# A two-block model in one program: no products of zeros ahead of the experts, and the six key and value units made among the experts all taken from the second layer

## The reference, cut to what matters

```
def hierarchical_moe(h, ...):                       # 256 tokens, D = 1024, 32 experts of 512
    y = jnp.zeros((B * S, D), jnp.float32)
    for e in range(N_EXPERTS):
        hid = jax.nn.silu(t @ w1[e]) * (t @ w3[e])
        y = y + comb[:, e:e + 1] * (hid @ w2[e]).astype(jnp.float32)

def memory_cross_attention(h, mem_n, w_q, w_kv, w_o):
    q = (h @ w_q).reshape(B, S, XATTN_HEADS, XATTN_HEAD_DIM)
    k, v = jnp.split(mem_n @ w_kv, 2, axis=-1)      # 256 x 1024 each, per layer
    ...

for l in range(DEPTH_2):                            # two layers
    x = x + FFN_RES_WEIGHT * swiglu_ffn(...)
    proj = rms_norm(x, mix_norm_g[l]) @ w_mix_in[l]
    y_rwkv = rwkv7_time_mix(...)                    # 8 heads
    y_moba = moba_attention(q_m, k_m, v_m, rel_bias)# 8 heads, one block of 256
    x = x + jnp.concatenate([y_rwkv, y_moba], axis=-1) @ w_mix_out[l]
    x = x + memory_cross_attention(rms_norm(x, xattn_norm_g[l]), rms_norm(mem, mem_norm_g[l]), ...)
    x = x + FFN_RES_WEIGHT * swiglu_ffn(...)
```

## Time and profile before

| | us |
|---|---|
| median of 3 runs (2256.39 to 2260.35) | 2259.84 |
| the profiled execution's own time | 2262.87 |
| its span, first to last instruction | 2261.1 |
| PE busy in the span | 2184.8 (97%) |
| DVE busy | 1240.1 (55%) |
| ACT busy | 426.6 (19%) |
| experts, pair 0's first product to the last scatter | 353.6 to 837.6 |
| head loop of layer 0, first transpose to last value product | 1172.1 to 1195.9 |
| head loop of layer 1 | 1874.9 to 1898.7 |

### The profile page before, as it was taken

One profiled execution on the slowest core, in us unless ns is written; L12 is line 12 of the kernel. 1 busy time (PEld: TensorE's weight loads), 2 busy tenths in 40 slices (PEclk: granted clock), 3 DMA queues, 4 the chain that ended last, 5 costly groups with the idle time before them and its releaser, 6 DMA issues.

```text
span 2261.1 us, 29957 instructions
## 1 busy us (share of the span) xinstructions
PE 2184.8 (97%) x12564; PEld 1481.3 (66%) x12564; DVE 1240.1 (55%) x2258; ACT 426.6 (19%) x858; POOL 50.5 (2%) x85
## 2 busy tenths in 40 slices
PE   7999999999999989999999999999999999999998
PEld 5778853433333337866968678856884976687873
DVE  2798422101110126676777766667666867767675
ACT  1123321101000012101142321101210132322110
POOL 1000100000000000000000000000000000000000
PEclk9999999999999999999999999999999999999999
DMA  9655587999999995444341435436453423245441
GB/s 406 266 223 232 223 277 303 421 421 421 422 421 421 421 390 161 163 168 167 113 163 45 149 122 174 162 130 214 159 181 135 168 83 125 78 151 182 159 181 42
DMA packets 174318, 499.98 MB, mean 221 GB/s; under 512 B 7128, under 2 KB 99560, under 8 KB 143984
## 3 DMA queue, kind: packets, MB, share of 16 engines
q1 hardware_dynamic: 169664, 481.23, 56.3%
q0 software_dynamic: 4384, 16.43, 2.2%
q10 hardware_dynamic: 144, 0.52, 0.1%
HBM read 491.34 MB, written 6.82 MB: 220 GB/s over the span
## 4 chain that ended last, share of the span: by engine, by line
PE 85%; DMA 9%; DVE 4%; ACT 1%; issue 1%; SPq 0%; POOL 0%; DVEq 0%; POOLq 0%
PE bank L2510 23%; PE bank L2558 11%; DMA ring<-in_w 8%; PE bank L1528 6%; PE bank L952 6%; PE bank L2623 6%; PE bank L1569 3%; PE bank L3053 2%; PE bank L2871 2%; PE bank L3126 2%; PE bank L1619 2%; PE bank L942 1%; PE bank L1056 1%; PE bank L1087 1%; PE bank L2602 1%; PE bank L1553 1%
## 5 line engine op out<-in xcount | busy, mean ns | idle before, releaser
L2510 PE MATMUL bank<-Tw,Sx 128*128 128x256 f32 x1032 | 229.9, 379 | 0.0
L2510 PEld LDWEIGHTS bank<-Tw,Sx 128*128 128x128 f32 x1032 | 193.0, 190 | 24.6
L1989 DVE TENSOR_TENSOR sg<-sg,bank 128x512 f32<-128x512 f32 x16 | 11.0, 688 | 283.4 <-PE bank L1528 283.4
L2510 PE MATMUL bank<-ring,xT 128*128 128x256 f32 x688 | 155.5, 379 | 0.0
L2510 PEld LDWEIGHTS bank<-ring,xT 128*128 128x128 f32 x688 | 130.5, 190 | 18.0 <-issue 0.5
L952 PE MATMUL bank<-xT,ring 128*128 128x256 f32 x640 | 141.8, 380 | 0.0
L952 PEld LDWEIGHTS bank<-xT,ring 128*128 128x128 f32 x640 | 120.7, 190 | 19.0 <-issue 3.3
L1528 PE MATMUL bank<-ring,xg 128*64 128x512 f32 x512 | 114.5, 594 | 18.5 <-DMA ring<-in_w 18.5
L1569 PE MATMUL bank<-ring,hTg 128*64 128x512 f32 x512 | 113.4, 595 | 0.0
L3550 DVE TENSOR_TENSOR whole<-bank,part 128x256 f32<-128x256 f32 (+1 forms) x133 | 57.5, 432 | 99.5 <-PE bank L2510 98.4
L2558 PE MATMUL bank<-Tw,Sx 128*128 128x512 f32 x240 | 108.9, 592 | 0.0
(11 more groups left out here) (643 smaller groups left out, 3761.6 us busy)
## 6 DMA issues: line engine op xcount, KB each, us to landing
ring<-in_w SPq DMA_DIRECT2D x128, 1024.0 KB, 23.9
ring<-in_ffn_w_in SPq DMA_DIRECT2D x88, 1024.0 KB, 7.7
ring<-in_first_pieces SPq DMA_DIRECT2D x33, 2048.0 KB, 11.9
more<-in_w SPq DMA_DIRECT2D x48, 1024.0 KB, 23.6
ring<-in_ffn_w_out SPq DMA_DIRECT2D x20, 2048.0 KB, 7.8
ring<-in_w_mix_in SPq DMA_DIRECT2D x12, 2048.0 KB, 7.9
ring<-in_xattn_w_kv SPq DMA_DIRECT2D x5, 2048.0 KB, 7.9
spare<-in_w SPq DMA_DIRECT2D x8, 1024.0 KB, 26.3
```

What stands on the lines that cost most here:

```text
L2510: last = nc.tensor.matmul(bank[BANK_OF[name]][:, 0:SEQ], lhs(k), rhs(k), start=(k == 0), stop=(k == 3))
```

## The change

`EARLY` now holds units 0 to 5 of layer 1, at steps 2 to 7. So `LEFT` becomes (0, 1, 2, 3, 6, 7) for layer 0 and (6, 7) for layer 1. `ALONE` is 4 in layer 0 and 2 in layer 1: layer 0 has one more whole unit ahead of the head loop and two units in it, where it had one; in layer 1 the second unit is the one in two halves, around `bonus` and the two `mats`, and the head loop has none. Layer 0 loads three pieces of `xattn_w_kv`, layer 1 one (before, two and two). Step 0 of the experts is written out apart on PE without anything to scatter in pair 0; the first scatter, in pair 1, opens the banks itself (`start=True`).

```diff
-EARLY = ((0, 0, 1), (0, 1, 2), (1, 0, 3), (1, 1, 4), (1, 2, 5), (1, 3, 6))
+EARLY = ((1, 0, 2), (1, 1, 3), (1, 2, 4), (1, 3, 5), (1, 4, 6), (1, 5, 7))
...
-            pe.wait_ge(kv_act, 2)
-            pe.wait_ge(ye_dve, 2)
-            for b in range(4, 8):
-                last = nc.tensor.matmul(bank[b][:, :], ye[:, 0, 0:P], ye[:, 1, :], start=True, stop=False)
-            last.then_inc(scattered, 1)
-            for lo, hi, first, l, keys in EARLY_SEGMENTS:
+            for q in range(2):
+                up(0, q)
+                if q == 1:
+                    pe.wait_ge(ye_dve, 2)
+                    gather(1, 0, (0, 1))
+                    scatter(0, 0, 0, start=True)
+                turn(0, q)
+                if q == 1:
+                    scatter(0, 1, 1)
+                    pe.wait_ge(hT_ready, 2)
+                    pe.wait_ge(whotT_ready, 2)
+                    gather(1, 1, (2, 3))
+                down(0, q)
+            for lo, hi, first, l, keys in EARLY_SEGMENTS[1:]:
...
-            for half in range(2):
-                nc.vector.memset(ye[:, half, :], 0.0).then_inc(ye_dve, 1)
-            nc.vector.memset(whotT[:, 1, :], 0.0).then_inc(whotT_ready, 1)
             weighted(0)
...
-        ALONE = [4 if len(t) > 4 else 3 for t in LEFT]
+        ALONE = [4 if len(t) > 4 else len(t) // 2 + 1 for t in LEFT]
...
                 scores(0)
-                cross_kv(l, LEFT[l][1])
+                cross_kv(l, LEFT[l][1], range(0, KD if ALONE[l] > 2 else 4))
                 bonus(l)
                 if ALONE[l] == 4:
                     cross_kv(l, LEFT[l][2])
                 pe.wait_ge(fac_ready, l + 1)
                 mats(l, 0)
-                cross_kv(l, LEFT[l][ALONE[l] - 1], range(0, 4))
+                if ALONE[l] > 2:
+                    cross_kv(l, LEFT[l][ALONE[l] - 1], range(0, 4))
                 mats(l, 2)
                 cross_kv(l, LEFT[l][ALONE[l] - 1], range(4, KD))
```

More of the change, by code:

```diff
@@ L150 @@
         EARLY_SEGMENTS.append((_i, _i + 1, _u, _l, _g < 4))
-_full, _at = [], 0
+_full, _at = [(0, 1, None, None, None)], 1
+assert EARLY[0][2] > 0
 for _s in EARLY_SEGMENTS + [(PAIRS // 2, PAIRS // 2, None, None, None)]:
@@ L1511, in up @@
                 for m in range(2):
-                    if m == 1:
-                        pe.wait_ge(whotT_ready, n + 1)
+                    if m == 1 and not (isinstance(n, int) and n == 0):
+                        pe.wait_ge(whotT_ready, n)
                         if taken is not None:
@@ L1545, in turn, with scatter @@
                 last.then_inc(whotT_psum, 1)
-            def scatter(par, turn_, done, stop=False):
-                pe.wait_ge(scattered, done)
+            def scatter(par, turn_, done, start=False, stop=False):
+                if start:
+                    pe.wait_ge(kv_act, 2)
+                else:
+                    pe.wait_ge(scattered, done)
                 for e in range(2):
@@ L1553, in scatter @@
                         last = nc.tensor.matmul(bank[4 + 2 * t + half][:, :], whotT[r, par, t * P:(t + 1) * P],
-                                                ye[r, half, :], start=False, stop=stop)
+                                                ye[r, half, :], start=start, stop=stop)
                 last.then_inc(scattered, 1)
@@ L1601, in tensor_gathered @@
                         if first is not None and q == 0:
-                            pe.wait_ge(whotT_ready, n + 2)
+                            pe.wait_ge(whotT_ready, n + 1)
                             early_products(pe, xT, i + (first - lo + 1), l, keys)
-            pe.wait_ge(whotT_ready, PAIRS + 1)
-            pe.wait_ge(ye_dve, 2 * PAIRS + 2)
+            pe.wait_ge(whotT_ready, PAIRS)
+            pe.wait_ge(ye_dve, 2 * PAIRS)
             for turn_ in range(2):
-                scatter((PAIRS + 1) % 2, turn_, 2 * PAIRS + turn_ + 1, stop=turn_ == 1)
+                scatter((PAIRS + 1) % 2, turn_, 2 * PAIRS + turn_ - 2, stop=turn_ == 1)
             for _ in range(6):
@@ L2002, in vector_gathered @@
                 if t == 0:
-                    dve.wait_ge(scattered, 2 * PAIRS + 3)
+                    dve.wait_ge(scattered, 2 * PAIRS)
                 for half in range(2):
@@ L2074, in build @@
         KEYS_LEFT = [sum(g < 4 for g in t) for t in LEFT]
-        KV_PLACES = [{4: (0, 1, 2, 3), 3: (0, 1, 3), 2: (0, 3)}[len(t) // 2] for t in LEFT]
+        KV_PLACES = [{4: (0, 1, 2, 3), 3: (0, 1, 3), 2: (0, 3), 1: (0,)}[len(t) // 2] for t in LEFT]
         assert all(t[0::2] == [g - 1 for g in t[1::2]] for t in LEFT)
@@ L3313, in take_kv @@
                     nc.scalar.activation(dst, bank[g % 2][:, :], ACT.Copy).then_inc(kv_act, 1)
-                for g in LEFT[l][0:2]:
+                ahead = 2 if ALONE[l] > 2 else 1
+                for g in LEFT[l][0:ahead]:
                     take_kv(g)
@@ L3318, in mixer @@
                 expo(1)
-                for g in LEFT[l][2:ALONE[l]]:
+                for g in LEFT[l][ahead:ALONE[l]]:
                     take_kv(g)
```

8 lines of the change are left out of this document (4 added, 4 removed).

## The result

The changed kernel takes 2275.77 us (median of 4 runs, 2274.06 to 2279.3) against 2259.71 for the kernel before; ratio 1.0076, 95% interval 1.0063 to 1.0089: **16 us slower**. The forecast was 2269.3 (2261.5 to 2275.5). The sign was right; the loss is 16.1 us where +9.5 was worked out, 0.3 us past the range. The profiled execution has its own time 2279.3, span 2277.5, against 2262.87 and 2261.1.

A forecast was written before the change was run, and what follows sets the result against it. Weights bound the experts; elsewhere PE, or PE and DVE in turn. Experts -1.2, layer 0's mixer +11.2 and layer 1's -0.5 sum to +9.5 us on the median 2259.84: 2269.3 us, range 2261.5 to 2275.5.

The forecast's parts named there:

- Start of the experts: Pair 0's first `up`, without zero products, starts 4.1 us earlier; half clock loses 1.7, so transfers resume 2.4 us earlier.
- End of the experts: Step 7's added unit makes PE end the experts 1.25 us later, turning the start's 2.4 us gain into -1.2 us.
- Layer 0's mixer: Two more units cost +6.5 us ahead of the head loop and +4.7 in it, +11.2 together (9 to 14.1).
- Layer 1's mixer: Two units fewer give -1.5 us, a fallen clock costs 1.0, so -0.5 us (ends -1.5 and +5.1).
- -1.5 with the clock held: Layer 1's mixer: what losing two units gains at full clock, since DVE bounds the stretch ahead of the loop.
- I take 1.0 us: Layer 1's mixer: the loss assumed for falls of the clock of 3.4 us in the emptied engine's waits.
- signs of being wrong: Layer 1's `turned(0)` distance shrinking by a unit, layer 0's loop not growing, or half clock over most of layer 1's loop.
- The argument that small products hold the clock: Against the clock falling through layer 1's loop: the inverse behind it, also small products, holds its clock.
- The rule of the Trainium skill: Transposes don't count as clock work and idle gaps are bad, so layer 1's loop would stay low: the +5.1 end.
- Rival 1: The clock falls through layer 1's loop: +5.1 there in place of -0.5, +15.1 in all, 2274.9 us; chance 0.16.
- Rival 2: A unit costs the same wherever it stands; layer 1 gives back 11.7 us, -1.7 in all, 2258 us; chance 0.10.
- rival 3: Start of experts: `xg` late for another reason, no gain; +11.9 in all, 2271.7 us; 0.70 together with the forecast.

The follow-up runs named there:

- e3: The changed kernel plus 12 products that nobody reads, ahead of layer 1's five longest waits: 2268.3 us, ratio 1.0048 to the kernel before.
- e2: The kernel before with the new table of units and new mixers, its products of zeros kept: 2272.4 us, ratio 1.0062.
- e11: The kernel before plus 51 products (204 instructions) in a branch not taken, so only addresses move: 2264.2 us, ratio 1.0021.
- e8: The changed kernel plus 24 never-run products, three unread products ahead of the first `up`, and 12 in layer 1's waits: 2265.4 us, ratio 1.0033.
- e10: e6 plus three unread products ahead of the first `up`, with four units of layer 0 and two of layer 1 made early: 2271.2 us, ratio 1.0058.
- e1: The changed kernel with the old table of units and the mixers as before, still without zero products: 2261.7 us, ratio 1.0015 to the kernel before.
- e6: e1 plus 24 products in the branch not taken, which never run and only move addresses: 2257.9 us, ratio 0.9996.
- e5: e1 plus four products in the branch not taken, which never run and only move addresses: 2258.0 us, ratio 0.9998.

## Why the prediction was right or wrong

- **Start of the experts: right in mechanism and nearly in size.** `up` at 349.37 (349.5 forecast), half clock for the 3.4 us assumed, transfers 2.57 us earlier (2.4). That the clock fell was likely, not certain: in e3, whose code is the same there, it held.
- **End of the experts: the term was too dear.** The +1.25 for the unit in step 7 rested on the second `up` running without waits from a fixed 801.9, and it did run so; but step 7's first `down` came 4.57 us earlier, not 2.4; why it gained 2.0 us more than the transfers did at the start isn't shown. Experts without zero products take 476.1 to 479.2 us with the old table (six traces) and 477.1 to 479.1 with a unit in step 7 (four): the +1.25 is not to be seen. With zero products it was 482.34, 480.02 and 479.17, so the profile shown before lies high, by 1.7 us of clock under its own zero products (5.37 us there, 3.67 in e2 and e11) and by 0.6 to 1.5 that have no cause here. Means of three and of ten traces give -2.6 for the whole stage where -1.2 was forecast.
- **Layer 0's mixer: right.** +10.8 measured, +11.2 forecast, with both parts in place: +6.1 ahead of the loop, +4.7 in it, one wait of 0.56 left of 2.39. Three kernels repeat it.
- **Layer 1's mixer: one term of two mis-sized.** "-1.5 with the clock held" is what e3 and e8 measure. "I take 1.0 us" for the clock is 4.4 in the changed kernel, 4.6 in e2, and 6.5 in layer 0 of e10 (if -1.5 holds there too). The working took falls of 3.4 us, the first mostly under a wait; there were two, of 6.8 and 17.1 us, the second over 13.5 of the loop's 24.7 us and the two groups of products behind it. So one of the prediction's own signs of being wrong came, half clock over most of layer 1's loop. To the first product behind the loop, where its sum ends, the layer is +1.3 (51.98 against 50.69); the two groups behind it, which it left out, add 1.6. The argument that small products hold the clock, from the inverse behind the loop, did not carry over: the inverse, with no wait above 0.8 us, ran at 1.00, the loop, with waits of 1.7 to 2.5 us, did not. e3 put dense products into those waits, so it shows that filling them holds the clock, but not whether the waits or the want of dense products let it fall. The rule of the Trainium skill that was set against the row there ("TensorE: Matmul & The Clock Gate", Part 4 and "Why this matters for your kernels") was the better guide in its direction: the loop did fall to 1.2 GHz. No run tells its two parts, transposes and gaps, from each other. Rival 1 gave +5.1 for this layer; the changed kernel shows +2.9, and the three kernels that leave a layer two units 2.9 to 5.0. Rival 1's total, 2274.9, is 0.9 us from the measured time, but by luck: what it has too much in layer 1 the pause makes up.
- **Rival 2 is out** (a unit is worth the same in either layer: it costs 5.4 where it is added and gives back 0.75 where it is removed, with the clock held), and so is rival 3 (`xg` was ready).
- **The step that failed is one that wasn't there.** The sum held everything between the experts and layer 0's mixer at nothing, without a reason. The pause and its clock put +4.9 there; by whole times it is 3.8 (medians of e1 and e6) to 4.7 (e11's ratio). Without it the changed kernel would be at about 2271, an estimate from the 4.9, inside the range; layer 1's clock, 1.0 where 4.4 was measured, is the second step, and experts 2.0 us shorter than forecast hid part of both. The pause can't be read from the kernel's logic, only from where a jump lands; with it (+4.9), layer 1 (+3.4), the experts (-2.0), layer 0 (-0.4) and the rest (+1.0) the forecast's +9.5 becomes 16.4, the difference of the spans.

## What to carry to other kernels

Where two engines take turns, a filler is worth its time only on the side that has none to spare; moved away from a stage that the other engine bounds, it gives back almost nothing (1.5 us for two units here) and can take the clock along, and products that nobody reads may then make the stage faster. When an edit moves code ahead of a taken branch, look for an "issue" pause in the first instructions behind the branch before blaming the edit: padding that never runs tells in one run. And compare stages, not totals, when executions of like code differ by 4 us before the place in question is reached.

## What the runs showed of the hardware

- Behind the jump over a branch not taken, TensorE paused for 2.0 to 3.7 us with 1 to 9 transposes ahead of the pause and went on 3.8 to 4.3 us after the first of them, in five kernels; in eight it did not pause. 16 instructions that never run took the pause away (e5), 204 brought it (e11). That it waits for its next block of instructions is read from this, from the count of 256 and from the transfer that begins 2.4 to 2.6 us before it goes on.
- A pause has a second price: with the half clock behind it, the stage took 4.7 to 6.3 us more than the 16.12 of traces with neither.
- A wait of the same length ahead of the same work lowers the granted clock in one execution and not in another: first `up` 8.78 us four times and 7.09 once behind 3.1 to 3.2 us; sixteen transposes 2.4 us or 3.2 to 3.3 behind 2.27 us. With the wait filled to 0.5 to 0.7 us the `up` took 7.09 in all five kernels.
